# Two seven-product schemes extended: the row-kept 256-column groups of the first projection, and the last of the first experts

## The chip, the cores and the metric

One core of a Trainium2 chip runs the whole program. The metric is the device time of one execution in microseconds. A core has a matrix engine (TensorE, PE in the profile, with PEld for its weight loads), a vector engine (VectorE, DVE), a scalar engine (ScalarE, ACT), GpSimd (POOL) and a queue engine (SyncE, SP), which run their own instruction streams and meet at semaphores. Sixteen DMA engines move data; the transfers that SP issues are in one hardware queue (q1), those of GpSimd in a software queue (q0).

## The reference

The program computes two transformer-like layers over 2048 rows of width 1024, in float32. Two places matter here. In the first layer a projection feeds attention and a recurrence:

```python
hx = modulate(rmsnorm(x, norm1_w), sh1, sc1)          # 2048 rows
hc = modulate(rmsnorm(ctx, norm1_w), csh1, csc1)      # 256 context rows
aq, ak, av, mq, mk, mv, mo, gates = split(h @ w_in)   # widths 512 128 128 512 512 512 512 16
```

Its last step is a mixture of 16 experts; each takes the 256 rows that score highest for it:

```python
xg = h[bidx, idx]                       # 16 experts x 256 rows x 1024
g = einsum('becd,edf->becf', xg, w_gate); u = einsum('becd,edf->becf', xg, w_up)   # f = 512
y = einsum('becf,efd->becd', silu(g) * u, w_down) * gate[..., None]
out = zeros_like(h).at[bidx, idx].add(y)
```

The second layer begins with a projection of the result by `w_in_2` (1472 columns).

## The kernel before

**The scheme.** A product of two matrices, each cut into 2 by 2 blocks, can be made of seven block products instead of eight, with sums and differences of blocks made by DVE before (`make_left`, `make_right`) and joined after (`join`). The code names them P1 to P7. P1 is copied out of PSUM by ACT, the others are added by DVE onto what is already in SBUF; P7 is added twice.

**First projection** (`first_projection`, L427). Nine turns of 256 rows (two tiles j of 128) run: turn 0, seven "fast" turns (`fast_body`, L989 for PE and L758 for DVE) and the context turn. A turn makes 8 units of 256 columns by column (`fm`, L1006), kept by ACT, and then column groups kept by row, `TM1`: group 0 (512 columns), 1 (256), 2 (512), 3 (272, with the gates) and 4 (256). In the fast turns groups 0 and 2 are the two column halves of a seven-product scheme over the two row tiles and the two depth halves (L1014), four depth steps a product; groups 1, 3 and 4 are plain products of eight depth steps for each row tile (L1018), copied out by DVE (`keep_step`, L751). The order on PE is `STEPS` (L447). Three PSUM banks (`NB = 3`) serve all units in rotation, so that a step waits until the step three before it has been taken; the first three units of the next turn wait until all row-kept results of this turn are taken (L998). DVE's order is written out by hand: norm of the next rows, rotation of the previous turn's attention rows (`rotate`, L617), left and right blocks, and then the joins and copies with the eight convolutions of the previous turn (`convolve`, three instructions each, L705 and L707) and two additions of a modulation product (L398) between them. The right blocks lie in `right` and in the weights, where turn 0 overwrites group 0 of depth half 0 with `t3` at its end (L835). The context turn (`body`, L1030) makes four column units, and then groups 1, 2 and the gates for each tile.

**First experts** (`experts`, L3014). Expert 0 and expert 15 (`LAST`) are plain (`plain_up`, `plain_down`); experts 1 to 14 use seven products for gate and up (L3247, 3.57 us each) and seven for down (L3276, `down`). Beside the up products PE transposes the next expert's rows (L3202). GpSimd scatters each expert's two tiles of 128 rows into x with an accumulating indirect DMA (L3180). The blocks' scratch lies in the memory of the second projection's weights, `inp2_w`: SP loads these (`EarlyColumns.load`, L337, 5.9 MB in four transfers) once expert 14 is done (L3144). When the scatters have landed the stage ends with a barrier, and the second projection begins by loading rows of x, and waits for its weights at L4192 and L4167.

Of the kernel before, what the change touches and what calls it, by code (L numbers as in the profile page):

```python
# [10 lines left out]
ALU = mybir.AluOpType  # L11
# [317 lines left out]
class EarlyColumns:  # L329
# [7 lines left out]
    def load(self, sp):  # L337
        for k in range(0, KD, 4):
            sp.dma_start(self.w[:, k:k + 4, self.first:], self.view[:, k:k + 4, self.first:]).then_inc(self.fm_landed, 16)
        for k in range(0, KD, 4):  # L340
            sp.dma_start(self.w[:, k:k + 4, 0:self.first], self.view[:, k:k + 4, 0:self.first]).then_inc(self.tm_landed, 16)
# [85 lines left out]
def first_projection(nc, K, groups, first_weights, late_mod, rope, q_norm, k_norm, taps, tm_out, qT_out, kT_out, conv_out, tm_k,  # L427
# [18 lines left out]
    P1, P2, P6, P5, P3, P7, P4 = "P1", "P2", "P6", "P5", "P3", "P7", "P4"  # L446
# [3 lines left out]
    kept_order = [P2, (0, 1), (0, 3), (0, 4), (1, 1), P3, P7, (1, 3), (1, 4), P4]  # L450
    joined_order = [P6, P5, P7]
# [30 lines left out]
    with Stage(nc, "inp1") as s:  # L482
# [11 lines left out]
        left = s.sb("left", [P, 2, KH, P])  # L494
        o = s.sb("o", [P, TB, W])
# [16 lines left out]
                 "first_kept", "joined", "t3_made", "right_made", "left_made", "zeroed", "edged", "cch", "conved", "silued", "scaled", "y_stored", "k_turned", "k_kept", "k_stored", "gated", "passed")  # L512
        (dch, rooted, x_scaled, turned, hT_ready, unit, fm_kept, tm_kept,
         w_ready, squared, summed, q_rooted, qch, rotated, q_turned, q_kept, q_stored,
         first_kept, joined, t3_made, right_made, left_made, zeroed, edged, cch, conved, silued, scaled, y_stored, k_turned, k_kept, k_stored, gated, passed) = (s.sem(n) for n in names)
# [4 lines left out]
        b11, t3, b21, b22 = (w[:, depth * KH:(depth + 1) * KH, lo:lo + BANK]  # L520
                             for depth, lo in ((0, tm_chunks[2][0]), (0, tm_chunks[0][0]), (1, tm_chunks[2][0]), (1, tm_chunks[0][0])))
# [5 lines left out]
        def joint(j, c):  # L527

            return tm[:, j, tm_at[c]:tm_at[c] + BANK]

        def step_bank(step):
            return psU[:, step_at[step] % NB, :]
# [4 lines left out]
        def wait_taken(engine, g, step):  # L537

            if step == P1:
                engine.wait_ge(first_kept, g)  # L540
            elif step in joined_order:
                engine.wait_ge(joined, g * 3 - 3 + joined_order.index(step) + 1)
            else:
                engine.wait_ge(tm_kept, g * NT + kept_order.index(step) + 1)
# [59 lines left out]
        def _(dve):  # L604
# [107 lines left out]

            def make_left(g, par, n):
# [15 lines left out]
            def make_right(g, n):  # L729

                at_g = g * 4 - 4
                if n == 2:
                    dve.wait_ge(t3_made, 1)
                    ins = dve.tensor_tensor(right[:, :, :], t3, b11, ALU.add)
                else:
                    dve.wait_ge(right_made, at_g + (1 if n == 1 else 3))
                    ins = dve.tensor_tensor(right[:, :, :], b22 if n == 1 else b21, right[:, :, :], ALU.subtract)
                ins.then_inc(right_made, 1)

            def join(g, step, to, other, after, done):  # L740

                wait_made(dve, g, step)
                if after:
                    wait_taken(dve, g, after)
                dve.tensor_tensor(to, step_bank(step), other, ALU.add).then_inc(done, 1)  # L745

            def keep_step(g, step):
                j, c = step
                lo, n = tm_chunks[c]
                wait_made(dve, g, step)  # L750
                dve.tensor_copy(tm[:, j, tm_at[c]:tm_at[c] + n], step_bank(step)[:, 0:n]).then_inc(tm_kept, 1)  # L751
# [6 lines left out]
            def fast_body(g, par, following):  # L758
# [9 lines left out]
                dve.wait_ge(tm_stored[0], g * 16)  # L768
                join(g, P2, joint(0, 2), joint(1, 2), P1, tm_kept)
                convolve(b, other, 0)  # L770
                join(g, P6, joint(1, 2), joint(1, 2), P1, joined)
                make_right(g, 1)
                make_left(g, par, 4)
                keep_step(g, (0, 1))
                convolve(b, other, 1)
# [3 lines left out]
                dve.wait_ge(tm_stored[1], g * 16)  # L779
                join(g, P5, joint(1, 0), joint(1, 2), P6, joined)  # L780
                make_left(g, par, 3)
                keep_step(g, (0, 4))
                make_right(g, 2)
                keep_step(g, (1, 1))
                convolve(b, other, 3)
                make_right(g, 4)
                join(g, P3, joint(0, 0), joint(1, 0), P5, tm_kept)
                keep_gates(g, 0)
                convolve(b, other, 4)
                mod.add(dve, g + 1, 1, psT[:, 1, :])  # L790
                join(g, P7, joint(1, 0), joint(1, 0), P5, tm_kept)
                join(g, P7, joint(1, 2), joint(1, 2), P6, joined)
                convolve(b, other, 5)
                keep_step(g, (1, 3))
                convolve(b, other, 6)
                keep_step(g, (1, 4))
                convolve(b, other, 7)
                join(g, P4, joint(1, 2), joint(1, 2), P7, tm_kept)
# [3 lines left out]
            def body(g, par, following):  # L802
# [31 lines left out]
                if first_turn(g):  # L834
                    dve.tensor_tensor(t3, b22, t3, ALU.subtract).then_inc(t3_made, 1)  # L835
# [10 lines left out]
        def _(act):  # L846
# [58 lines left out]
            def body(g, par, following):  # L905
# [17 lines left out]
                if fast(g):  # L923
                    act.wait_ge(tm_stored[1], g * 16)
                    wait_made(act, g, P1)
                    act.activation(joint(1, 2), step_bank(P1), ACT.Copy).then_inc(first_kept, 1)
# [21 lines left out]
        def _(pe):  # L948
# [40 lines left out]
            def fast_body(g, par, following):  # L989
                lhs = {P1: rows_of(par, 0, 0), P2: rows_of(par, 1, 0), P6: left[:, 1, :, :], P5: left[:, 0, :, :],  # L990
                       P3: left[:, 1, :, :], P7: left[:, 0, :, :], P4: rows_of(par, 1, 1)}
                rhs = {P1: b11, P2: b21, P6: right[:, :, :], P5: right[:, :, :], P3: b22, P7: t3, P4: right[:, :, :]}
                pe.wait_ge(hT_ready, g * TB * 2 + TB * 2)
                for u in range(UW):
# [13 lines left out]
                    elif step in lhs:  # L1008
                        if step in (P6, P3, P7):
                            pe.wait_ge(left_made, g * 4 - 4 + {P6: 2, P3: 3, P7: 4}[step])  # L1010
                        if step in (P6, P5, P4):
                            pe.wait_ge(right_made, g * 4 - 4 + {P6: 1, P5: 2, P4: 4}[step])
                        for k in range(KH):
                            mm = pe.matmul(psU[:, u % NB, :], lhs[step][:, k, :], rhs[step][:, k, :], start=(k == 0), stop=(k == KH - 1))  # L1014
                    else:
                        j, (lo, n) = step[0], tm_chunks[step[1]]
# [4 lines left out]
                    if u + 1 in MOD_AFTER:  # L1021
                        r = MOD_AFTER.index(u + 1)
# [7 lines left out]
            def body(g, par, following):  # L1030
# [4140 lines left out]
```

## Time and profile before

| what | us |
|---|---|
| median of 3 runs (lowest, highest) | 3951.31 (3942.11, 3953.16) |
| the profiled execution's own time | 3947.6 |
| span of the profile | 3946.0 |
| PE busy | 3646.0 (92%) |
| DVE busy | 2497.9 (63%) |
| ACT busy | 1554.6 (39%) |
| mean granted TensorE clock | 0.964 of full |

The page gives the shares over the whole span; stages differ, so the views by stretch of time are what the argument rests on. In them each row is one instruction or a run of equal ones: start, duration, engine, line of the kernel, operation, what it writes and reads, count, and in brackets how long the engine had been idle before it and what ended the wait. Two starts on one engine give the time that a thing really takes up, since the durations of neighbours overlap by some hundredths.

### The profile page before, as it was taken

The page shows a single profiled execution, that of the slowest core. Times are in us where ns is not written, and L with a number is a line of the kernel's source. Part 1 is how long each engine was busy: PE and PEld are TensorE (multiplying, and loading weights), DVE is VectorE, ACT ScalarE, POOL GpSimd, SP SyncE. Part 2 cuts the span into 40 slices and gives each one's busy share as a digit, 9 for nine tenths or more (in the row PEclk, how much of TensorE's full clock was granted, in tenths as well). Part 3 has the DMA queues.
Part 4 walks back from the last instruction along what each step waited for, and adds up shares of the span by engine and source line. Part 5 has one row for each costly group of instructions (what it writes and reads, how often), then busy time and mean ns, then how long its engine had stood idle before and what let it go on. Part 6 is the DMA issues. An engine that isn't in the chain of part 4 may idle for free. (4 is left out here: it accounts for less than half of the span.)

```text
span 3946.0 us, 65209 instructions
## 1 busy us (share of the span) xinstructions
PE 3646.0 (92%) x22959; PEld 2415.7 (61%) x22960; DVE 2497.9 (63%) x4701; ACT 1554.6 (39%) x3424; POOL 682.2 (17%) x802
## 2 busy tenths in 40 slices
PE   6999999699898977999999899998999999599998
PEld 4667776455594434888787677765666555344444
DVE  1456556556488754787874487785333566678886
ACT  1122221355563432222121467664333233367765
POOL 0000000100173220212120010110000132322222
PEclk8999999899999988999999899998999999699999
DMA  6122222222435568767664221224240143598974
GB/s 247 67 91 85 73 90 70 90 74 82 126 121 188 174 251 314 226 203 225 215 214 152 68 66 62 64 65 122 67 133 16 37 153 118 211 325 267 332 240 101
DMA packets 227211, 574.59 MB, mean 146 GB/s; under 512 B 28154, under 2 KB 100986, under 8 KB 211118
## 3 DMA queue, kind: packets, MB, share of 16 engines
q1 hardware_dynamic: 177742, 395.92, 28.6%
q0 software_dynamic: 49248, 175.79, 15.3%
q8 instruction: 130, 2.13, 0.2%
q14 instruction: 91, 0.75, 0.1%
HBM read 433.59 MB, written 137.93 MB: 145 GB/s over the span
## 5 line engine op out<-in xcount | busy, mean ns | idle before, releaser
L4959 DVE COPY moe_bu<-moe_wu 128x1024 f32 x480 | 298.9, 698 | 38.8 <-DMA moe_wd<-in_w_down 21.7
L4846 PE MATMUL moe_psU<-moe_bu,shared_weights 128*32 128x256 f32 x3840 | 295.1, 382 | 1.4 <-issue 1.3
L4846 PE MATMUL moe_psU<-moe_wu,shared_weights 128*32 x1280 | 293.2, 382 | 1.5 <-DVE moe_bu L4959 1.3
L4175 PE MATMUL inp_psU<-shared_weights,inp_w 128*128 128x256 f32 x1024 | 231.9, 382 | 2.8 <-DMA inp_wg<-in_lru_wx 2.8
L4175 PEld LDWEIGHTS inp_psU<-shared_weights,inp_w 128*128 128x128 f32 x1024 | 195.1, 192 | 35.8 <-issue 10.2
L4915 ACT ACTIVATE moe_bd<-moe_wd 128x1024 f32 x200 | 198.0, 1048 | 28.8 <-PE moe_psD L4868 28.8
L4846 PEld LDWEIGHTS moe_psU<-moe_wu,shared_weights 128*32 128x32 f32 x1280 | 134.3, 110 | 111.5 <-issue 12.5
L1006 PE MATMUL inp_psU<-inp_hT,inp_w 128*128 128x256 f32 x896 | 197.2, 380 | 5.5 <-DVE inp_tm L745 4.9
L1006 PEld LDWEIGHTS inp_psU<-inp_hT,inp_w 128*128 128x128 f32 x896 | 168.7, 190 | 32.9 <-DVE inp_tm L745 6.4
L1501 DVE TENSOR_SCALAR_CACHE_REDUCE att_junk<-att_psS,att_snk 128x640 f32<-128x640 f32 x128 | 108.1, 882 | 108.8 <-PE att_psS L1420 108.8
L4868 PE MATMUL moe_psD<-moe_bd,moe_hT 128*32 128x512 f32 x960 | 153.2, 595 | 0.0
L1018 PE MATMUL inp_psU<-inp_w,inp_hT 128*128 128x256 f32 (+1 forms) x672 | 152.6, 384 | 0.0
L4846 PEld LDWEIGHTS moe_psU<-moe_bu,shared_weights 128*32 128x32 f32 x3840 | 151.2, 110 | 1.6 <-issue 1.6
L4868 PE MATMUL moe_psD<-moe_wd,moe_hT 128*32 x320 | 151.1, 595 | 1.1 <-ACT moe_hT L4912 0.5
L3180 POOL DMA_INDIRECT x<-moe_y,moe_at_out x32 | 68.3, 2136 | 482.2 <-DVE moe_y L3467 414.8
L1547 ACT ACTIVATE att_p<-att_psS,att_low 128x640 f32<-128x640 f32 x128 | 101.3, 793 | 119.2 <-DVE att_junk L1501 97.8
L1018 PEld LDWEIGHTS inp_psU<-inp_w,inp_hT 128*128 128x128 f32 x672 | 126.6, 190 | 25.4 <-issue 6.7
L4898 ACT ACTIVATE shared_weights<-moe_psT,mod_cols,mod_scale 128x128 f32<-128x128 f32 x320 | 120.4, 458 | 48.9 <-PE moe_psT L4834 48.9
L3457 DVE TENSOR_TENSOR inp_w<-moe_ps,inp_w 128x512 f32<-128x512 f32 x84 | 58.1, 692 | 104.4 <-PE moe_ps L3247 102.9
L3313 ACT ACTIVATE moe_xT<-moe_psT,mod_cols,mod_scale 128x128 f32<-128x128 f32 x256 | 95.5, 457 | 70.9 <-PE moe_psT L3202 70.8
L4502 ACT ACTIVATE lata_pT<-lata_psP 128x512 f32<-128x512 f32 (+3 forms) x112 | 61.2, 549 | 157.7 <-PE lata_psP L4402 157.7
L4451 DVE TENSOR_TENSOR lata_psS<-lata_psS,lata_mask 128x128 f32<-128x128 f32 x64 | 19.0, 297 | 159.4 <-PE lata_psS L4392 159.4
(805 smaller groups left out, 8590.5 us busy)
## 6 DMA issues: line engine op xcount, KB each, us to landing
moe_wu<-in_w_up SPq DMA_DIRECT2D x32, 2048.0 KB
moe_d_w<-in_w_down SPq DMA_DIRECT2D x16, 2048.0 KB, 13.2
moe_wd<-in_w_down SPq DMA_DIRECT2D x32, 1024.0 KB
moe_u_w<-in_w_up SPq DMA_DIRECT2D x15, 2048.0 KB, 14.0
mod_w<-in_w_ada SPq DMA_DIRECT2D x24, 1024.0 KB, 12.0
inp_mod_w<-in_w_mod SPq DMA_DIRECT2D x16, 1024.0 KB, 4.8
xn<-out_xn POOLq DMA_DIRECT2D x32, 512.0 KB, 4.4
shared_weights<-in_w_gate SPq DMA_DIRECT2D x8, 2048.0 KB, 8.9
```

Source lines behind the costliest of these rows:

```text
L1006: mm = pe.matmul(psU[:, u % NB, 0:G], w[:, k, fm_lo + u * P:fm_lo + (u + 1) * P], hT[:, par, k, :], start=(k == 0), stop=(k == KD - 1))
L1018: mm = pe.matmul(psU[:, u % NB, 0:n], hT[:, par, k, j * P:(j + 1) * P], w[:, k, lo:lo + n], start=(k == 0), stop=(k == KD - 1))
L1501: dve.tensor_scalar(junk[:, kv, :], psS[:, kv, LO:LO + KEYS], 1.0, snk[:, 1, h:h + 1], ALU.mult, ALU.min, accum_out=low[:, j, h:h + 1]).th ...
L1547: act.activation(p[:, g % 2, kv, :], psS[:, kv, LO:LO + KEYS], ACT.Exp, scale=-1.0, bias=low[:, j, h:h + 1], accum_out=sums[:, j, h:h + 1] ...
L3180: pool.indirect_dma_start(out=target, out_offset=bass.IndirectOffsetOnAxis(ap=at_out[:, p, r:r + 1], axis=0), in_=y[:, p, r, :], in_offset ...
L3313: ins = act.activation(xT[:, e % 2, k, r * P:(r + 1) * P], psT[:, h, (k % 4) * P:(k % 4 + 1) * P], ACT.Identity, scale=scale2[k], bias=shi ...
L4175: mm = pe.matmul(psU[:, m % 2, u % 2 * G:(u % 2 + 1) * G], w[:, k, TM2_W + u * P:TM2_W + (u + 1) * P], hT[:, par, k, :], start=(k == 0), s ...
L4846: mm = pe.matmul(psU[c, f, 0:2 * P], xT[:, p, k, c], w, start=(k == 0), stop=(k == KD - 1), tile_position=(0, g * LOT))
L4868: mm = pe.matmul(psD[c, n, :], hT[:, f, c], w, start=(f == 0), stop=(f == FB - 1), tile_position=(0, g * LOT))
L4898: ins = act.activation(xT[:, p, k, :], psT[:, q, (k % 4) * P:(k % 4 + 1) * P], ACT.Identity, scale=scale2[k], bias=shift2[k])
L4915: return act.activation(bd[:, g - 1, f, :].unsqueeze(1), wd[:, bass.ds(slot, 1), f, :], ACT.Copy)
L4959: ins = dve.tensor_copy(bu[:, g - 1, f, c, :].rearrange("p k n -> p (k n)").unsqueeze(1), wu[:, bass.ds(slots[g - 1], 1), f, c, :].rearran ...
```

## The change

In the fast turns of the first projection groups 1 and 4 become the column halves of a second seven-product scheme (`SLIM`, 256 columns a half) beside the first one (`WIDE`, 512). Its right blocks take the place of the rotation's scratch `qsq`, and its `t3` overwrites group 4 of depth half 0; the gates' 16 columns of the region read by the context turn are saved before and put back in the context turn, whose row-kept units wait for it. DVE's order is new. In the experts the last one also uses seven products, and the second projection's weights are loaded in two halves by depth, the first when the last expert's up products are done, the second when its down products are.

```diff
-    STEPS = [P1, P2, P6, (0, 1), (0, 3), P5, (0, 4), (1, 1), P3, P7, (1, 3), (1, 4), P4]
+    STEPS = [(P1, WIDE), (P2, WIDE), (P1, SLIM), (P2, SLIM), (P6, WIDE), (P6, SLIM), (0, 3), (P5, WIDE), (P5, SLIM), (1, 3),
+             (P3, WIDE), (P3, SLIM), (P7, WIDE), (P7, SLIM), (P4, WIDE), (P4, SLIM)]
+    MOD_FAST = (NF + 4, NF + 12)
...
+        rights = right[:, :, :], qsq[:, :, :].rearrange("p j n -> p (j n)")[:, 0:KH * 256].rearrange("p (k n) -> p k n", k=KH)
+        t3_gates = t3[SLIM][:, :, 240:256]
...
-                make_right(g, 2)
+                make_right(g, WIDE, 2)
+                make_right(g, SLIM, 2)
                 dve.wait_ge(fm_kept, g * NF + NF)
                 edges(b, other, False)
...
+                join(g, (P2, WIDE), 0, 0, 0, tm_kept, P1)
                 convolve(b, other, 0)
+                join(g, (P2, SLIM), 0, 0, 0, tm_kept, P1)
+                join(g, (P6, WIDE), 1, 0, 0, joined, P1)
+                make_right(g, WIDE, 1)
+                join(g, (P6, SLIM), 1, 0, 0, joined, P1)
+                make_right(g, SLIM, 1)
                 make_left(g, par, 4)
                 keep_step(g, (0, 3))
                 mod.add(dve, g + 1, 0, psT[:, 0, :])
+                join(g, (P5, WIDE), 1, 1, 0, joined, P6)
+                convolve(b, other, 1)
+                join(g, (P5, SLIM), 1, 1, 0, joined, P6)
+                make_left(g, par, 3)
+                make_right(g, WIDE, 3)
+                keep_step(g, (1, 3))
+                make_right(g, WIDE, 4)
+                join(g, (P3, WIDE), 0, 1, 1, tm_kept, P5)
+                make_right(g, SLIM, 3)
+                make_right(g, SLIM, 4)
+                join(g, (P3, SLIM), 0, 1, 1, tm_kept, P5)
+                dve.wait_ge(tm_kept, g * NT + kept_order.index((P3, SLIM)) + 1)
+                keep_gates(g, 0)
                 convolve(b, other, 2)
+                join(g, (P7, WIDE), 1, 1, 1, tm_kept, P5)
+                join(g, (P7, WIDE), 1, 0, 0, joined, P6)
                 convolve(b, other, 3)
+                join(g, (P7, SLIM), 1, 1, 1, tm_kept, P5)
+                join(g, (P7, SLIM), 1, 0, 0, joined, P6)
+                mod.add(dve, g + 1, 1, psT[:, 1, :])
                 convolve(b, other, 4)
                 convolve(b, other, 5)
+                join(g, (P4, WIDE), 1, 0, 0, tm_kept, P7)
                 convolve(b, other, 6)
+                join(g, (P4, SLIM), 1, 0, 0, tm_kept, P7)
                 convolve(b, other, 7)
...
                     rotate(g - 1, 1 - par)
+                    dve.tensor_copy(t3_gates, gates_quadrant[:, :, :]).then_inc(quadrant_saved, 1)
...
+                    dve.tensor_tensor(t3[WIDE], b22[WIDE], t3[WIDE], ALU.subtract).then_inc(t3_made, 1)
+                    dve.tensor_copy(gates_quadrant[:, :, :], t3_gates).then_inc(quadrant_saved, 1)
+                    dve.wait_ge(quadrant_saved, 1)
+                    dve.tensor_tensor(t3[SLIM], b22[SLIM], t3[SLIM], ALU.subtract).then_inc(t3_made, 1)
...
+                    act.wait_ge(rotated, g * 4 * TB)
+                    for pair in (WIDE, SLIM):
+                        wait_made(act, g, (P1, pair))
+                        act.activation(joint(pair, 1, 0), step_bank((P1, pair)), ACT.Copy).then_inc(first_kept, 1)
...
+                    if u == NF and is_ctx(g):
+                        pe.wait_ge(quadrant_saved, 2)
...
     def plain(e):
-        return e in (0, LAST)
+        return e == 0
...
-            sp.wait_ge(made, base(LAST))
-            next_columns.load(sp)
+            sp.wait_ge(made, made_by(LAST, P4))
+            next_columns.load_half(sp, 0)
+            sp.wait_ge(made, made_by(LAST, P4, True))
+            next_columns.load_half(sp, 1)
...
-            for e in range(1, LAST):
+            for e in range(1, units):
                 up(e)
                 down(e)
-            plain_up(LAST)
-            plain_down(LAST)
```

## Rows read from the trace of the kernel before

**Rows 1.** The page: PE's busy time, share of the span and instructions.

```profile
PE 3646.0 (92%) x22959; PEld 2415.7 (61%) x22960; DVE 2497.9 (63%) x4701; ACT 1554.6 (39%) x3424; POOL 682.2 (17%) x802
```

**Rows 2.** One fast turn by windows: length, busy time of each engine, clock, DMA share, GB/s.

```profile
375.00:454.92 79.92, 79.14 (x331) 56.70 (x331) 46.66 (x87) 18.32 (x39) 5.00 (x8) 1.00 0.23 83
```

**Rows 3.** Timeline of PE in that turn, and the next turn's first row.

```profile
412.66 3.60 PE L1014 MATMUL inp_psU<-inp_right,inp_left 128*128 128x512 f32 x8
416.09 3.62 PE L1018 MATMUL inp_psU<-inp_w,inp_hT 128*128 128x256 f32 x16
419.64 1.06 PE L388 MATMUL inp_psT<-inp_mod_w,inp_mod_cb 128*32 128x512 f32 x8
...
450.54 3.60 PE L1014 MATMUL inp_psU<-inp_right,inp_hT 128*128 128x512 f32 x8
454.92 10.63 PE L1006 MATMUL inp_psU<-inp_hT,inp_w 128*128 128x256 f32 x48 [0.78 <-DVE inp_tm L745]
```

**Rows 4.** Timeline of DVE in the same turn.

```profile
404.22 0.17 DVE L695 COPY inp_fm<-inp_fm 128x8 f32<-128x8 f32 x1 [5.23 <-ACT inp_fm L913]
...
416.90 2.28 DVE L737 TENSOR_TENSOR inp_right<-inp_w,inp_right 128x2048 f32<-128x2048 f32 x1
...
419.75 0.43 DVE L751 COPY inp_tm<-inp_psU 128x256 f32<-128x256 f32 x1
420.09 0.35 DVE L705 TENSOR_SCALAR inp_y<-inp_fm,inp_tap 128x256 f32<-128x256 f32 x1
...
441.02 0.35 DVE L705 TENSOR_SCALAR inp_y<-inp_fm,inp_tap 128x256 f32<-128x256 f32 x1
...
442.33 0.68 DVE L398 TENSOR_TENSOR inp_mod_row<-inp_mod_row,inp_psT 128x512 f32<-128x512 f32 x1
443.62 1.29 DVE L745 TENSOR_TENSOR inp_tm<-inp_psU,inp_tm 128x512 f32<-128x512 f32 x2 [0.61 <-PE inp_psU L1014]
...
454.17 0.69 DVE L745 TENSOR_TENSOR inp_tm<-inp_psU,inp_tm 128x512 f32<-128x512 f32 x1 [1.71 <-PE inp_psU L1014]
```

**Rows 5.** Timeline of the context turn: PE's first row-kept unit.

```profile
710.92 3.62 PE L1068 MATMUL inp_psU<-inp_w,inp_hT 128*128 128x256 f32 x16
```

**Rows 6.** Timeline of the context turn: DVE, the rotation's last and a later copy.

```profile
713.35 0.22 DVE L652 TENSOR_TENSOR inp_o<-inp_t 128x64 f32<-128x64 f32 x1
...
734.60 0.69 DVE L822 COPY inp_tm<-inp_psU 128x512 f32<-128x512 f32 x1 [1.66 <-PE inp_psU L1068]
```

**Rows 7.** Timeline of PE: expert 14 (first rows), start of expert 15.

```profile
2087.53 7.31 PE L3247 MATMUL moe_ps<-moe_xT,shared_weights 128*128 128x128 f32 x64
2094.67 0.60 PE L3202 MATMUL moe_psT<-ident,moe_xg 128*128 128x128 f32 x4
2095.11 3.74 PE L3247 MATMUL moe_ps<-inp_w 128*128 128x128 f32 x32
...
2126.30 3.62 PE L3224 MATMUL moe_ps<-moe_xT,moe_g_w 128*128 128x256 f32 x16
```

**Rows 8.** Timeline of POOL: expert 14's second scatter, expert 15's second.

```profile
2129.40 1.55 POOL L3180 DMA_INDIRECT x<-moe_y,moe_at_out  x1 [1.95 <-DVE moe_y L3467]
...
2170.62 1.55 POOL L3180 DMA_INDIRECT x<-moe_y,moe_at_out  x1 [5.33 <-DVE moe_y L3370]
```

**Rows 9.** Timeline of SP and PE: the second projection's first rows.

```profile
2177.77 0.82 SPq L3638 DMA_DIRECT2D shared_rows<-x  x2
...
2192.89 20.00 PE L4175 MATMUL inp_psU<-shared_weights,inp_w 128*128 128x256 f32 x80 [2.79 <-DMA inp_wg<-in_lru_wx]
```

**Rows 10.** DMA issues near the end of expert 13: size, us from issue to landing.

```profile
moe_d_w<-in_w_down SPq DMA_DIRECT2D x1, 2048.0 KB, 12.8
x<-moe_y,moe_at_out POOLq DMA_INDIRECT x1, 10.6
```

**Rows 11.** DMA issues, 2080 to 2200 us: the second projection's weights.

```profile
inp_w<-in_w_in SPq DMA_DIRECT2D x2, 896.0 KB, 20.5
```

**Rows 12.** DMA issues, 2169 to 2173 us: the last scatter.

```profile
x<-moe_y,moe_at_out POOLq DMA_INDIRECT x1, 5.9
```

More of the change, by code:

```diff
@@ L335, in __init__, with load_half @@
         self.fm_landed, self.tm_landed = nc.alloc_semaphore(f"{name}_fm_landed"), nc.alloc_semaphore(f"{name}_tm_landed")
[L337 to L341, printed above, removed]
+    def load_half(self, sp, n):
+        k = 4 * n
+        sp.dma_start(self.w[:, k:k + 4, self.first:], self.view[:, k:k + 4, self.first:]).then_inc(self.fm_landed, 16)
+        sp.dma_start(self.w[:, k:k + 4, 0:self.first], self.view[:, k:k + 4, 0:self.first]).then_inc(self.tm_landed, 16)
 class LateModulation:
@@ L537, in wait_taken @@
         def wait_taken(engine, g, step):
[L539 to L542, printed above, removed]
+            if step[0] == P1:
+                engine.wait_ge(first_kept, g * 2 - 1 + step[1])
+            elif step in joined_order and step not in kept_order or step[0] == P7:
+                engine.wait_ge(joined, g * 6 - 6 + joined_order.index(step) + 1)
             else:
@@ L711, in convolve @@
                 ins.then_inc(conved, 1)
+            right_order = [(WIDE, 2), (SLIM, 2), (WIDE, 1), (SLIM, 1), (WIDE, 3), (WIDE, 4), (SLIM, 3), (SLIM, 4)]
             def make_left(g, par, n):
@@ L727, in make_left, with make_right, join @@
                 ins.then_inc(left_made, 1)
[L729 to L734, printed above, removed]
[L735 to L737 removed]
+            def make_right(g, pair, n):
+                at_g = g * 8 - 8 + right_order.index((pair, n))
+                to = rights[pair]
+                if n in (2, 3):
+                    dve.wait_ge(t3_made, pair + 1)
+                    ins = dve.tensor_tensor(to, t3[pair], b11[pair], ALU.add)
+                else:
+                    dve.wait_ge(right_made, g * 8 - 8 + right_order.index((pair, n - 1 if n == 4 else 2)) + 1)
+                    ins = dve.tensor_tensor(to, b22[pair] if n == 1 else b21[pair], to, ALU.subtract)
                 ins.then_inc(right_made, 1)
[L740 removed]
+            def join(g, step, j, half, other, done, after):
+                pair = step[1]
                 wait_made(dve, g, step)
[L743 to L745 removed]
+                if after == P1:
+                    dve.wait_ge(first_kept, g * 2 - 1 + pair)
+                else:
+                    dve.wait_ge(joined, g * 6 - 6 + joined_order.index((after, pair)) + 1)
+                dve.tensor_tensor(joint(pair, j, half), step_bank(step), joint(pair, 1, other), ALU.add).then_inc(done, 1)
             def keep_step(g, step):
[L748 to L749 removed]
                 wait_made(dve, g, step)
[L751 removed]
+                dve.tensor_copy(tm[:, step[0], tm_at[3]:tm_at[3] + 272], step_bank(step)).then_inc(tm_kept, 1)
             def keep_gates(g, j):
@@ L764, in fast_body @@
                 make_left(g, par, 2)
-                make_right(g, 2)
+                make_right(g, WIDE, 2)
+                make_right(g, SLIM, 2)
                 dve.wait_ge(fm_kept, g * NF + NF)
                 edges(b, other, False)
-                dve.wait_ge(tm_stored[0], g * 16)
-                join(g, P2, joint(0, 2), joint(1, 2), P1, tm_kept)
+                for j in range(TB):
+                    dve.wait_ge(tm_stored[j], g * 16)
+                join(g, (P2, WIDE), 0, 0, 0, tm_kept, P1)
@@ L1124, in put_tm @@
             def put_tm(g, j):
-                pool.wait_ge(tm_kept, g * NT + (kept_order.index(P3) + 1 if fast(g) and j == 0 else (j + 1) * NC))
+                pool.wait_ge(tm_kept, g * NT + (kept_order.index((P3, SLIM)) + 1 if fast(g) and j == 0 else (j + 1) * NC))
                 hi = tm_at[3] if is_ctx(g) else TM1_W
@@ L3335, in _ @@
             silu_plain(0)
-            for e in range(1, LAST):
+            for e in range(1, units):
                 if e > 1:
@@ L3478, in _ @@
             make_x_right(1, 3)
-            for e in range(1, LAST):
+            for e in range(1, units):
                 keep_gates(e)
```

79 lines of the change are left out of this document (31 added, 48 removed).

## The prediction

> **What bounds the kernel now.** The page comes first: PE is busy for 92% of the span, DVE for 63% [rows 1]. The table by windows then shows whether this holds where the change is: in a fast turn of the projection PE works 79.14 of 79.92 us at the full granted clock, DVE 46.66 [rows 2]. Third, the timeline of PE: the only pause is 0.78 us at the turn's start, ended by DVE's last join, that of P4 [rows 3]. So a shorter PE turn shortens the kernel, as long as DVE stays behind PE by no more than it does now; what DVE has queued when PE ends a turn is what to look at. In the experts PE's work is one row after another [rows 7] until the last expert; after it comes no PE work but a chain: last weighing on DVE, scatter by GpSimd, landing, barrier, loading of rows [rows 8, 9].
>
> **PE in a fast turn.** Removed are four plain products: the 16 instructions of one take 419.64 - 416.09 = 3.55 us from start to start, 0.222 each [rows 3]; four are 14.20. Added are seven slim products of 8 such instructions, 1.775 each: 12.43. PE's work shrinks by 1.77 us. Seven wide products (3.43 each, 416.09 - 412.66) stay. PE would end P4 SLIM at 450.54 + 3.43 - 1.77 = 452.20, on the old turn's scale.
>
> **DVE's tail.** Going backwards from 452.20: P4 SLIM 1.77, P4 WIDE 3.43, P7 SLIM 1.77, so P7 WIDE ends at 445.23 and its join starts 0.2 later (the old P4's: ended 453.97, join at 454.17 [rows 3, 4]), at 445.4. From there DVE has, in its written order, the following. Two wide joins: 1.29 for both, less overlap 1.21. One convolution: 442.33 - 441.02 = 1.31. Two slim joins: a copy of 256 columns out of PSUM takes 0.34 from start to start and 0.43 in itself; the trace has no slim join, so I take the copy's 0.34, since a wide join's 0.69 is what a 512-column addition [rows 4] takes too; 0.68. The modulation's addition 0.60 (0.68 less overlap). Two convolutions 2.62. The wide P4 join 0.61. One convolution 1.31. That adds up to 8.34: the last join starts at 453.75 and ends after 0.43 at 454.18; PE starts 0.06 after such an end (454.17 + 0.69 = 454.86 against 454.92). The new turn begins at 454.24, not 454.92: 0.68 us are gained, and PE idles 2.04 us in place of 0.78. Convolutions 4 to 6 stand between PE's last products and the joins that release the next turn; before, DVE had 1.71 us of idleness there [rows 4]. Seven turns give **4.8 us**.
>
> Does DVE arrive at 445.4 in time? P3 WIDE ends at 441.8 - 1.0 (modulation product, 1.06 less overlap [rows 3]) - 1.77 = 439.0. Then follow its join (0.61, from 439.2), two slim right blocks, the P3 SLIM join, gates 0.3, one convolution. A slim right block has 1024 elements; between 0.69 for 512 and 2.28 for 2048 lies 1.22, less overlap 1.14. The sum ends at 444.0, so 1.4 us are spare. Further back, the wide right block (2.20) and then the slim join, slim right block and left block between P6 and P5 end about 426, while P5 SLIM begins about 430: covered. At the turn's front, DVE now idles 5.23 us before the edges [rows 4]; one slim block (1.14) and the convolution and gates that slip behind the last join (about 1.1 us later relative to PE) fit in. The turn-0 additions (copy and second t3, about 1.4 us) fit there too. If that cover were gone, PE would wait for P2's join by what exceeds it. ACT's later silu, one convolution later, delays only column units that have two banks in hand. The modulation's second product comes eight steps after the first, not four, with its load between, so it waits less.
>
> A rule of the Trainium skill speaks against the halves: "VectorE: DVE Perf Modes", section "The TRN2 errata", says that an instruction reading SBUF pays a fixed time whatever its size, and advises tiles of 512 or more. If each of the three slim joins in the tail cost its full 0.43, the turn would gain 0.4 and not 0.7 us, and the total below would be 2 us higher; the 0.34 from start to start is the trace's, and decides.
>
> **The context turn.** PE reaches its first row-kept unit at 710.92 without a wait [rows 5]. It now waits for the copy that puts the gates' columns back, which DVE issues behind the whole rotation; that ends at 713.57 [rows 6]. With 0.2 for the copy and 0.06 for the release, PE starts at 713.8: 2.9 us later. Behind it stand all its row-kept units, and DVE waits for them (1.66 us before the copy at 734.60 [rows 6]), so nothing gives it back. The bounds are 0 (only if DVE's other work were what bounds the end) and 3.5. I take **2.9 lost**.
>
> **The last expert.** Expert 14 takes 2126.30 - 2087.53 = 38.77 us of PE, of which four transposes (2095.11 - 2094.67 = 0.44 each, 1.76) fall away for the last [rows 7]: 37.0, so PE ends at 2163.3. The second scatter of expert 14 was issued 3.10 us after PE's end (2129.40 against 2126.30 [rows 7, 8]); so this one is issued at 2166.4, 4.2 us before the old 2170.62. The old one landed in 5.9 [rows 12], at 2176.5, and the stage ended 1.25 later with the first row loads at 2177.77 [rows 9]. But the second half of the weights, 2.94 MB, is now issued at about 2163.5, and a scatter beside such a load takes 10.6 us [rows 10]. That gives 2177.0, stage end 2178.25: **0.5 us lost**, where the PE side promised 4.2.
>
> The weights of the half: 2 MB beside two scatters landed in 12.8 [rows 10], or 0.25 MB/us with the scatters' 1.05 MB counted; all 5.9 MB, the last part issued at 2128, landed at 2148.5 with two scatters [rows 11], 0.31 MB/us. So 4 MB take 12.7 to 16 us and end at 2176 to 2179.7. The row loads are issued behind them in the same queue at 2178.25 and may start up to 1.4 us late; PE's first products had waited 2.79 us for another load [rows 9], which covers it. The bounds of this part are -4.2 (no slowing) and +4 (the half ends 4 us after my latest, beyond cover).
>
> The Trainium skill's "DMA: Bandwidth & Descriptors", section "Queues, rings and completion order", says that each DMA engine takes turns between the queues that have work, a packet at a time. With the two queues sharing evenly, a scatter of 5.9 us would take up to twice that, 11.8, and the stage would end 1.2 us later than by the 10.6 used here; the rows agree with the rule.
>
> **Sum.** 3947.6 - 4.8 + 2.9 + 0.5 = 3946.2 against the profiled execution's own time. That execution was 3.7 us under the median of the three runs; the same difference on the median gives 3949.9. I put the time between, at 3948.
>
> **Rivals.**
> *DVE keeps up.* If DVE's tail did not bind, the last join would start at 452.4, and the turn gain 454.92 - 452.85 = 2.07 us, 14.5 in all: 3947.6 - 14.5 + 2.9 + 0.5 = 3936.5, and 3931.8 if the scatter isn't slowed either. For it: DVE is idle 33 us a turn. Against: eight operations written between P7's end and P4's last join. Chance 0.20.
> *The scatter is not slowed,* the rest as forecast: 3947.6 - 4.8 + 2.9 - 4.2 = 3941.5. For it: the weights' first rows may be over when it starts. Against: rows 10. Chance 0.12.
> *Slower: slim operations on DVE cost as much as wide ones.* Then the two slim right blocks add 2 x 1.06, which uses up the 1.4 spare and starts the tail 0.7 late, and the slim joins add 2 x 0.27 + 0.26: the turn begins at 455.7, 0.8 later than before. It decides once the tail is over 0.7 longer than I have it. Seven turns lose 5.6, so 3947.6 + 5.6 + 2.9 + 0.5 = 3956.6, and 3960.6 with the late weights. Against: the copy of 256 takes 0.43, not 0.69. Chance 0.15.
> *The change doesn't shorten PE:* if a slim product took a wide one's 3.43, a turn would grow by 7 x 3.43 - 14.2 = 9.8: 4016. The 256-column row excludes nearly all of it. Chance 0.03.
> The forecast has 0.50.
>
> **How the numbers follow.** What can be told from no change is 0.3%, 11.8 us. The forecast, the quick scatter and most of the others lie within it: 0.77. Faster by more takes DVE keeping up and a bit beside: 0.15. Slower by more takes the slow rival with late weights, or the last: 0.08. The range, 3936 to 3957, goes from the first rival to the third, and holds what the runs of before spread.
>
> **What would show it.** In the changed profile: fast turns of about 79.2 us, with PE idle about 2 us at each start, ended by a DVE join, and DVE without a gap between P7's joins and P4's; PE idle near 3 us in the context turn before its first row-kept unit, ended by the copy of the gates' columns; a last expert of 37 us on PE, its last scatter landing in 10 to 11 us, and the second projection's first row load within a microsecond of where it was. I am wrong if the turns are 78 us (or 80 and more), or if that load comes 4 us earlier.

## The result and the profile after

| | before | changed |
|---|---|---|
| median of 20 runs of each | 3947.46 us | 3954.39 us |
| ratio, 95% interval | | 1.0016 [1.0009, 1.0023] |
| profiled execution: own time, span | 3947.6, 3946.0 | 3952.9, 3951.3 |

The change costs 4 to 9 us (the interval of the ratio) where the forecast said 1.4 less for the profiled execution. One run of the changed kernel took 6384.9 us at a mean granted clock of 0.61; it is not in the ratio, and without it the median is 3954.37. The line of the page that answers to [rows 1]; columns as there:

```profile
PE 3640.3 (92%) x22995; PEld 2411.2 (61%) x22996; DVE 2565.2 (65%) x4779; ACT 1557.7 (39%) x3431; POOL 685.3 (17%) x802
```

PE is busy 5.7 us less, and yet the kernel is longer. I went through both timelines by the same marks:

| stretch (us) | before | changed | difference | forecast |
|---|---|---|---|---|
| turn 1 to context turn, first product to first product | 558.78 | 557.89 | -0.9 | -4.8 |
| context turn, first product to first row-kept unit | 16.01 | 20.51 | +4.5 | +2.9 |
| from there to expert 15's first product | 1415.4 | 1417.5 | +2.1 | 0 |
| expert 15's start on PE to the second projection's row load | 51.47 | 51.80 | +0.3 | +0.5 |
| from that row load to the end of the span | 1768.2 | 1767.3 | -0.9 | 0 |

With 0.15 us ahead of turn 1 these make the 5.3 us of the spans. The last expert came out near the forecast (+0.3 for +0.5). The 0.9 us gained in the last stretch lie at its start: from the row load to the second projection's first product it takes 14.18 us, before 15.12. That product waited 2.79 us for another load before [rows 9]; now it waits 1.77 for ACT. The loss is in the projection. The timeline of PE in the changed kernel shows the projection's turns (start, length, engine, line, operation; in brackets the idle time before and who ended it):

```profile
294.00 10.63 PE L1037 MATMUL inp_psU<-inp_hT,inp_w 128*128 128x256 f32 x48 [1.90 <-DVE inp_tm L763]
373.32 12.31 PE L1037 MATMUL inp_psU<-inp_hT,inp_w 128*128 128x256 f32 x48 [1.90 <-DVE inp_tm L763]
454.32 10.63 PE L1037 MATMUL inp_psU<-inp_hT,inp_w 128*128 128x256 f32 x48 [1.90 <-DVE inp_tm L763]
533.72 12.29 PE L1037 MATMUL inp_psU<-inp_hT,inp_w 128*128 128x256 f32 x48 [1.99 <-DVE inp_tm L763]
694.17 8.83 PE L1098 MATMUL inp_psU<-inp_hT,inp_w 128*128 128x256 f32 x32 [2.00 <-DVE inp_tm L763]
...
714.68 5.41 PE L1102 MATMUL inp_psU<-inp_w,inp_hT 128*128 128x256 f32 x16 [2.64 <-DVE inp_w L834]
```

The turn from 294.00 takes 79.32 us, as forecast (79.24), with 1.90 idle at its start (2.04). But the 48 matmuls at 373.32 and 533.72 take 12.31 and 12.29 us and not 10.63; the 32 of the context turn take 8.83 where the kernel before has 7.14, and the 16 behind the new 2.64 us wait take 5.41 and not 3.62 [rows 5]. In four places the same instructions take longer, by 1.68, 1.66, 1.69 and 1.79: 6.8 us together. The table by windows says why (window, length, busy PE, granted clock, DMA share, GB/s):

```profile
373.30:375.00 1.70, 1.68 (x6) 0.79 0.00 0
375.00:377.00 2.00, 2.00 (x6) 0.50 0.74 303
377.00:380.00 3.00, 3.00 (x14) 0.88 0.09 30
453.00:458.00 5.00, 3.68 (x17) 1.00 0.29 120
...
696.20:698.20 2.00, 2.00 (x6) 0.50 0.33 133
716.50:718.50 2.00, 2.00 (x6) 0.50 0.00 0
```

The granted clock is at 0.50, the 1.2 GHz level, for a few microseconds shortly after the pause; there the matmuls start about twice as far apart. At 454, behind a pause as long, it stays at 1.00. In the kernel before it is 1.00 over the fast turn [rows 2], its start included.

### The profile page after: what moved, and what is told of

The parts are those of the page before. It is cut to its first block and busy times, and to the rows that moved or that the text cites. A ratio compares the mean times of both kernels' runs of the same rounds, so it can differ in the third digit from the quotient of the medians.

```text
span 3951.3 us, 65537 instructions
## 1 busy us (share of the span) xinstructions
PE 3640.3 (92%) x22995; PEld 2411.2 (61%) x22996; DVE 2565.2 (65%) x4779; ACT 1557.7 (39%) x3431; POOL 685.3 (17%) x802
## 5 line engine op out<-in xcount | busy, mean ns | idle before, releaser
L763 DVE TENSOR_TENSOR inp_tm<-inp_psU,inp_tm 128x512 f32<-128x512 f32 (+1 forms) x98 | 53.1, 554 | 132.4 <-PE inp_psU L1046 132.4
L4841 POOL DMA_INDIRECT out_rows<-shared_weights,moe_at_out x40 | 64.8, 1620 | 272.9 <-DVE shared_weights L4983 202.2
```

Source lines behind the costliest of these rows:

```text
L4841: pool.indirect_dma_start(out=out, out_offset=bass.IndirectOffsetOnAxis(ap=at_out[:, p, :], axis=0), in_=y[:, p, :], in_offset=None, compu ...
```

## The experiments

**The pause theory:** PE's new pauses of 1.9 to 2.6 us sometimes let the granted clock fall to 1.2 GHz for a few microseconds of work after, and that is what ate the gain. **Rivals:** the slim products themselves (their DVE work, their weight loads); the DMA load that runs there; DVE in arrears from turn to turn. The kernel before was run beside each batch: median 3949.51 beside the first four, 3946.78 beside the next four, 3947.84 beside the last two; so ratios are compared, and places within the profiles. A run's later stages vary by some microseconds (the output stage, from the first reload of its columns to the issue of the next modulation's weights, took 217.8 to 221.5 us in the twelve profiles, its code the same in all), which a median alone doesn't separate. The clock goes along with that too. Windows of that stage's start in two of the kernels below, first in both, where the stage is 3.1 us shorter, then in best; columns as above:

```profile
1186.00:1206.00 20.00, 16.46 (x36) 0.84 0.92 307
1206.00:1226.00 20.00, 16.99 (x45) 0.91 0.32 108
...
1246.00:1266.00 20.00, 16.82 (x68) 1.00 0.55 189
```

```profile
1186.00:1206.00 20.00, 16.99 (x36) 0.78 0.84 285
1206.00:1226.00 20.00, 16.68 (x39) 0.83 0.41 129
...
1246.00:1266.00 20.00, 16.61 (x60) 0.91 0.46 161
```

**tail.** On DVE the P4 join of the wide scheme is moved ahead of one convolution (5), that of the slim scheme ahead of two (5 and 6); convolution 7 stood behind both already:

```diff
                 mod.add(dve, g + 1, 1, psT[:, 1, :])
                 convolve(b, other, 4)
+                join(g, (P4, WIDE), 1, 0, 0, tm_kept, P7)
+                join(g, (P4, SLIM), 1, 0, 0, tm_kept, P7)
                 convolve(b, other, 5)
-                join(g, (P4, WIDE), 1, 0, 0, tm_kept, P7)
                 convolve(b, other, 6)
-                join(g, (P4, SLIM), 1, 0, 0, tm_kept, P7)
                 convolve(b, other, 7)
```

> The changed kernel with DVE's last convolutions (5, 6, 7) of a fast turn moved behind both P4 joins. Pause theory: a pause of 1.9 to 2.0 us of PE at a turn's start lets the granted clock drop to 0.5 in some turns (three of seven in the profile of the changed kernel), which costs 1.7 us each time. The pause shrinks by 1.33 to about 0.6 us, all seven starts are fast, turns take about 77.9 us: 3952.9 - 7 x 1.33 - 3 x 1.7 = 3938.5. Rival, slim products: the slow starts come from what PE computed before (the slim products), not from the pause: the pauses shrink, slow starts stay, 3943.6. Rival, backlog: the convolutions only push DVE's delay to the front of the next turn, PE waits there instead, no gain: 3952.

Measured 3940.45 (3938.34 to 3943.26), ratio 0.9981 [0.9972, 0.9990]. The turns are 77.9 us, and no start is slow. PE's timeline in it, a fast turn's start, the context turn's, and its first row-kept unit:

```profile
369.97 10.63 PE L1037 MATMUL inp_psU<-inp_hT,inp_w 128*128 128x256 f32 x48 [0.52 <-DVE inp_tm L763]
681.91 7.14 PE L1098 MATMUL inp_psU<-inp_hT,inp_w 128*128 128x256 f32 x32 [0.61 <-DVE inp_tm L763]
...
700.71 3.72 PE L1102 MATMUL inp_psU<-inp_w,inp_hT 128*128 128x256 f32 x16 [2.63 <-DVE inp_w L834]
```

The slim products are all there, and cost what PE's count said: 79.92 - 77.9 = 2.0 us a turn are gained, near the 2.07 of my rival "DVE keeps up". So neither they nor their DVE work are enough to make slow starts. The 2.63 us wait is still there and this time is followed by 3.72 us at a granted clock of 1.00: a pause makes a fall possible, not certain.

**copy_first.** The copy that puts the gates' columns back goes ahead of the rotation:

```diff
+                    dve.wait_ge(tm_kept, g * NT)
+                    dve.tensor_copy(t3_gates, gates_quadrant[:, :, :]).then_inc(quadrant_saved, 1)
                     rotate(g - 1, 1 - par)
-                    dve.tensor_copy(t3_gates, gates_quadrant[:, :, :]).then_inc(quadrant_saved, 1)
```

> The changed kernel with the copy of the gates' columns moved ahead of the rotation in the context turn. Pause theory: the wait of 2.64 us goes, and with it the slow first row-kept product (5.41 instead of 3.62 us): 4.4 us less, 3948.5. Rival, slim products or the context turn itself makes it slow: the product stays at 5.4, 2.6 us less, 3950.3. Rival, DVE bounds the context turn's end: nothing gained, 3952.9.

Measured 3951.55 (3948.57 to 3954.86), ratio 1.0007 [0.9998, 1.0016]. The first row-kept unit has no wait and full speed, 3.62 us; its place in the context turn moves from 20.51 to 17.70 us, and with the slow product the edit gives 4.6 us. By the medians (a ratio of 1.0007 against 1.0016) it is 3.6 us, which doesn't separate the 4.4 I expected from the 2.6 of the rival; the places do. The three slow starts at 373.95, 534.35 and 694.78, behind pauses of about 2 us, all stay:

```profile
694.78 8.83 PE L1099 MATMUL inp_psU<-inp_hT,inp_w 128*128 128x256 f32 x32 [1.99 <-DVE inp_tm L763]
...
712.48 3.62 PE L1103 MATMUL inp_psU<-inp_w,inp_hT 128*128 128x256 f32 x16
```

**pad.** The kernel before, without any slim product, with two more operations on DVE that only take time, so that PE waits longer at each turn's start:

```diff
                 convolve(b, other, 7)
+                for n in range(2):
+                    dve.tensor_tensor(qsq[:, :, :], qsq[:, :, :], qsq[:, :, :], ALU.max).then_inc(padded, 1)
+                    dve.wait_ge(padded, g * 2 - 1 + n)
                 join(g, P4, joint(1, 2), joint(1, 2), P7, tm_kept)
```

> The kernel before, without any slim product, with two additional DVE operations on 1280 elements (about 1.45 us each, values unchanged) ahead of the P4 join, so that PE's pause at each turn's start grows from 0.8 to about 2.0 us. Pause theory: the turns grow by 1.2 us, and some of the seven starts after them are slow, 1.7 us each: 3947.6 + 8.4 + 1.7 to 5.1 = 3957.7 to 3961. Rival, slim products: all starts stay fast: 3956.0.

Measured 3964.75 (3961.24 to 3969.07), ratio 1.0045 [1.0031, 1.0058]. The pauses are 2.04 to 2.29 us, and two of seven starts are slow:

```profile
300.12 10.63 PE L1009 MATMUL inp_psU<-inp_hT,inp_w 128*128 128x256 f32 x48 [2.19 <-DVE inp_tm L745]
381.45 12.21 PE L1009 MATMUL inp_psU<-inp_hT,inp_w 128*128 128x256 f32 x48 [2.19 <-DVE inp_tm L745]
```

So the kernel before does it too, given the pause. The rival of the slim products is out for a second time. The median is above the 3957.7 to 3961 that I had set: from the start at 218.78 to the context turn's the six turns take 11.4 us more than before (8.1 of pauses, 3.3 of two slow starts), and the rest of the difference is elsewhere and unexplained.

**projection_only.** The changes to the first projection without those to the experts.

> The first projection's part of the change alone, the experts as before. If the whole loss is in the projection, as the stage marks of the two profiles say (+5.5 us at the end of the projection, +0.3 in the experts): about 5 us over the kernel before, 3952.6. If the experts' part were what costs: 3947.

Measured 3949.62 (3945.47 to 3953.34), ratio 1.0003 [0.9994, 1.0012]. Its projection is the changed kernel's: slow starts at 373.88, 534.28, 694.71 and 715.21, and the last transposes of the modulation's row on PE 605.32 us after turn 1's start, 599.97 before, 5.35 more. The median shows next to nothing of these 5 us: the ratio is 1.3 per mille lower than the changed kernel's, and its interval includes 1. Part of that is later stages: from the second projection's row load to the end this profile took 1760.6 us, that of before 1768.2, of the changed kernel 1767.3. Whether all of it is, this run doesn't say.

**experts_only.** The experts' part alone.

> The kernel before with the experts' part of the change alone (the last expert like the others, the next weights in two halves). By my step: PE ends the last expert about 4 us earlier, but the last scatter lands in 10.4 us beside the second half of the weights instead of 5.9, so the row loads of the second projection are issued 0.3 to 0.5 us later than before: 3949.8 (3949 to 3951). Rival (the scatter isn't what sets the end of the stage): 4.2 less, 3945.3. Rival (late weights hold back the second projection's first rows): 2 to 4 us more there, 3952 to 3954.

Measured 3947.02 (3941.42 to 3950.45), ratio 1.0000 [0.9991, 1.0009]. From the issue of expert 14's gate weights, my mark for this stage, to the second projection's row load it takes 141.13 us, before 140.84: +0.3, as in the changed kernel (141.18). The last scatter in it lands in 10.3 us. The experts' part costs next to nothing and gives nothing.

**half_late.** The changed kernel, the second half of the weights only once the scatters have landed:

```diff
             sp.wait_ge(made, made_by(LAST, P4, True))
+            for p in range(2):
+                sp.wait_ge(stored[p], STORES * units // 2)
             next_columns.load_half(sp, 1)
```

> The changed kernel, with the second half of the next weights loaded only once all scatters have landed. If the load beside it is what stretches the last scatter, it lands in about 6.0 us instead of 10.4, and the stage ends some 4.3 us earlier in relation to PE's last product; then 2.94 MB of weights stand ahead of the row loads, 9.5 us at 0.31 MB/us, so that the second projection's first product comes about 3 us later than in the changed kernel: 3957. Rival (a scatter at the end takes 10 us whatever lies beside it): landing stays at 10.4, and the whole loses 7 us or more: 3962.

Measured 3952.22 (3947.38 to 3955.79), ratio 1.0013 [1.0003, 1.0022], against 1.0016 for the changed kernel; so the 3 us more that I expected of the whole don't show. In the place itself it is as expected. The last scatter by the DMA issues (kind and count, median us from issue to landing), first in the changed kernel, then here:

```profile
x<-moe_y,moe_at_out POOLq DMA_INDIRECT x1, 10.4
```

```profile
x<-moe_y,moe_at_out POOLq DMA_INDIRECT x1, 6.0
```

The row load comes 137.51 us after the same mark instead of 141.18, and the first product of the second projection 158.21 instead of 155.36, 2.9 later, behind the weights. The total doesn't show it, for which two things can stand: the two intervals overlap widely, and later stages were shorter in this profile (568.7 us from the last router's bias load to the end, 571.0 in the changed kernel's). This run has the changed kernel's projection unaltered, but its slow starts are at other turns:

```profile
291.84 12.31 PE L1037 MATMUL inp_psU<-inp_hT,inp_w 128*128 128x256 f32 x48 [1.90 <-DVE inp_tm L763]
372.84 10.63 PE L1037 MATMUL inp_psU<-inp_hT,inp_w 128*128 128x256 f32 x48 [1.90 <-DVE inp_tm L763]
452.15 12.31 PE L1037 MATMUL inp_psU<-inp_hT,inp_w 128*128 128x256 f32 x48 [1.90 <-DVE inp_tm L763]
...
612.63 12.29 PE L1037 MATMUL inp_psU<-inp_hT,inp_w 128*128 128x256 f32 x48 [2.00 <-DVE inp_tm L763]
693.70 7.14 PE L1098 MATMUL inp_psU<-inp_hT,inp_w 128*128 128x256 f32 x32 [2.00 <-DVE inp_tm L763]
```

It is again every second one. So what runs in a particular turn isn't the cause, nor are arrears that build up: those would come back in the same turn.

**both.** The edits of tail and copy_first together.

> The changed kernel with both earlier edits: P4's two joins ahead of convolutions 5 to 7 on DVE, and in the context turn the copy of the gates' columns ahead of the rotation. Pause theory: the turns stay at 77.9 us and their starts at 0.5 us of idleness; the 2.6 us pause in the context turn goes, and with it the half-clock product of 1.8 us behind it. Against P4's joins moved alone (3940.5) that is 4.4 less: 3936. From the context turn's start to the last modulation's mark it should take about 41.2 us, as before the change, and the x32 group at its start 7.14. Rival (the slow products belong to the slim products or to the load of the turn, not to pauses): a slow product stays in the context turn, 3938; if the pause merely moves to a later wait there, 3940.

Measured 3933.77 (3932.65 to 3936.23), ratio 0.9969 [0.9957, 0.9981]. All starts at full speed, the first row-kept unit 16.01 us into the context turn as before the change. This is faster than the kernel before by 7 to 17 us.

**filler.** The changed kernel; while PE would stand idle at a fast turn's end, it transposes the identity:

```diff
                         turn_q(g - 1, (u - NF - 1) // 2)
+                pe.wait_ge(q_kept, g * 3)
+                for n in range(12):
+                    mm = pe.transpose(psX[:, (n % 4) * P:(n % 4 + 1) * P], K["ident"][:, :], K["ident"][:, :])
```

> The changed kernel, and TensorE does 12 transposes of the identity (0.13 us each, 1.6 us) at the end of each fast turn, while it would stand idle for DVE's last join; their result is used nowhere. Nothing that the turn waits for is moved, so a turn stays at 79.3 us with 0.3 to 0.5 us of idleness instead of 1.9 to 2.0. Pause theory: what lowered the granted clock was TensorE standing still, so the starts of the turns at 373, 534 and of the context turn are no longer slow (10.6, 10.6 and 7.1 us instead of 12.3, 12.3 and 8.8): 5.1 less than the changed kernel, 3949.3; the slow product behind the 2.6 us pause in the context turn stays. Rival (the slow starts come from the turn's length or from what else runs then, not from the pause): all stay, 3954.4. Rival (the fillers come in the way of the last join or of the next turn): turns of over 79.6.

Measured 3949.82 (3945.17 to 3954.81), ratio 1.0004 [0.9995, 1.0013]. PE's timeline around a turn's start, at the context turn's, and its first row-kept unit:

```profile
213.42 1.47 PE L1063 MATMUL inp_psX<-ident 128*128 128x128 f32 x12
215.48 10.63 PE L1037 MATMUL inp_psU<-inp_hT,inp_w 128*128 128x256 f32 x48 [0.59 <-DVE inp_tm L763]
...
691.57 7.14 PE L1101 MATMUL inp_psU<-inp_hT,inp_w 128*128 128x256 f32 x32 [0.69 <-DVE inp_tm L763]
710.38 5.41 PE L1105 MATMUL inp_psU<-inp_w,inp_hT 128*128 128x256 f32 x16 [2.64 <-DVE inp_w L834]
```

This is the cleanest test: DVE's order, the transfers and the join that ends the wait are the changed kernel's, the turns stay at 79.3 us, and PE does more work. None of the seven starts is slow, and turn 1's start to the context turn's takes 554.50 us against 557.89: 3.4 less, and 1.69 more at the context turn's own start. The pause that wasn't filled, 2.64 us, is still followed by a slow product. The cause is PE standing still, not DVE's tail as such. By the ratios (1.0004 against 1.0016) the whole gains 4.7 us, near the 5.1 expected.

**pad_long.** As pad, with four operations in place of two.

> The kernel before with four extra DVE operations of 1.5 us (two in the earlier trial) in front of P4's join in each fast turn: 4.4 us more per turn than before, idleness at the start 5.1 us instead of 0.8. Seven turns add 30.5: 3980 without slow starts. Pause theory: every start behind so long a pause may be slow (1.7 us each), at least the 2 of 7 seen behind pauses of 2.1 us and up to all 8: 3983 to 3993. Rival (whether a start is slow hangs on the pause's place and not on its length): 2 slow again, 3983; rival (pauses have nothing to do with it): 3980.

Measured 3996.97 (3993.78 to 3999.63), ratio 1.0125 [1.0110, 1.0141]; more than any of the theories said. The pauses are 5.1 to 5.3 us, and all seven starts are slow; the timeline of the first and the longest of them, then the windows behind one pause:

```profile
219.61 12.94 PE L1009 MATMUL inp_psU<-inp_hT,inp_w 128*128 128x256 f32 x48 [5.09 <-DVE inp_tm L745]
...
392.33 13.61 PE L1009 MATMUL inp_psU<-inp_hT,inp_w 128*128 128x256 f32 x48 [5.24 <-DVE inp_tm L745]
```

```profile
651.90:655.90 4.00, 4.00 (x10) 0.50 0.58 225
655.90:657.90 2.00, 2.00 (x6) 0.52 0.99 342
657.90:660.90 3.00, 3.00 (x15) 1.00 0.06 21
```

The loss per start is 1.4 to 3.0 us. From 219.61 to the context turn's start at 739.10 the six turns take 519.5 us, 39.7 more than before: 26.4 of that are pauses (4.4 each), 13.3 the six slow starts. I had set 3983 to 3993, at most 1.7 a start; behind the longer pause the seven starts lose 2.2 on average.

**best.** Both DVE edits, and the next weights in three parts; some scratch blocks of the experts change places for it, which isn't shown here:

```diff
-            sp.wait_ge(made, made_by(LAST, P4))
-            next_columns.load_half(sp, 0)
-            sp.wait_ge(made, made_by(LAST, P4, True))
-            next_columns.load_half(sp, 1)
+            sp.wait_ge(made, made_by(LAST, P3))
+            next_columns.load_part(sp, 0, 4)
+            sp.wait_ge(mixed, 2 * LAST)
+            next_columns.load_part(sp, 4, 6)
+            sp.wait_ge(made, made_by(LAST, P3, True))
+            sp.wait_ge(d_right, 4 * LAST)
+            next_columns.load_part(sp, 6, 8)
```

> Both DVE edits, and the next weights in three parts by depth (4, 2 and 2 of the 8 blocks), issued in the last expert after the up product P3, behind the mixing, and after the down product P3. The projection's part as in the kernel with both DVE edits, 3936. In the last expert less is left to load when the last scatter starts (2 of 8 blocks, 1.5 MB, and it issued some us ahead, not 2.9 MB), so it should land in 6 to 8 us instead of 10.4: 3 to 4 us less, 3932.6. Rival (a scatter is slowed by whatever is loading when it starts, however little is left): 3936.

Measured 3929.36 (3922.80 to 3932.46), ratio 0.9953 [0.9939, 0.9967]: 13 to 24 us faster than the kernel before. The last scatter by the DMA issues, then SP's second and third part and the row load in its timeline:

```profile
x<-moe_y,moe_at_out POOLq DMA_INDIRECT x1, 6.3
```

```profile
2143.39 0.37 SPq L338 DMA_DIRECT2D inp_w<-in_w_in  x1
...
2150.45 0.37 SPq L338 DMA_DIRECT2D inp_w<-in_w_in  x1
...
2164.43 0.81 SPq L3672 DMA_DIRECT2D shared_rows<-x  x2
```

The third part is issued 6.3 us ahead of the last scatter (2156.79), and its two transfers land in 4.8 us (1024 KB) and 5.6 us (448 KB): it is over when that starts. The row load comes 137.15 us after the issue of expert 14's gate weights (141.23 in both), 4.1 less, and the second projection's first product 151.98 against 155.38: 3.4 gained, since that product now waits 2.47 us for another load.

## Why the prediction was wrong

- **PE in a fast turn, right.** Tail's turns gain 1.99 us where PE's count alone gave 2.07 (2.03, with the 0.43 of the last join and the 0.06 behind it added as in my own sum).
- **DVE's tail, right.** DVE's timeline in the changed kernel has no gap from P7's joins at 285.25 to P4's last, and my sum of it is right to within 0.1 us. The last join was to start 8.34 us after the first:

```profile
285.25 1.29 DVE L763 TENSOR_TENSOR inp_tm<-inp_psU,inp_tm 128x512 f32<-128x512 f32 x2 [1.02 <-PE inp_psU L1046]
...
287.76 0.75 DVE L763 TENSOR_TENSOR inp_tm<-inp_psU,inp_tm 128x256 f32<-128x256 f32 x2
...
291.63 0.68 DVE L763 TENSOR_TENSOR inp_tm<-inp_psU,inp_tm 128x512 f32<-128x512 f32 x1
...
293.53 0.42 DVE L763 TENSOR_TENSOR inp_tm<-inp_psU,inp_tm 128x256 f32<-128x256 f32 x1
```

  It starts 8.28 after. The slim joins cost 0.33 from start to start, the wide ones 0.60 to 0.61; the rival of dear slim operations is out, and half the columns cost little more than half the time.
- **"0.68 us are gained, and PE idles 2.04 us in place of 0.78": the step that failed.** I priced the idle time at its own length, and put what it does to the work behind it at nothing, without a reason. In the changed kernel's profile three of seven such pauses are followed by a stretch at 1.2 GHz that costs another 1.7 us: 3.4 in the seven turns, 1.7 at the context turn's start. Without that the seven turns give 4.2 us of my 4.8; with it 0.9 is left.
- **The context turn, right in its wait (2.64 against 2.9), short by the same thing.** The product behind that pause takes 1.8 us more, at a granted clock of 0.50; no term of the sum had it.
- **The last expert, right.** +0.3 for +0.5, the scatter in 10.4 us for 10.6; half_late and best show that the load beside it is what stretches it. So my rival of the scatter that isn't slowed is out.
- **The sum.** My 3946.2 and 6.8 of slow clock make 3953.0; the profile has 3952.9. That this agrees to 0.1 is partly luck: the 0.9 us gained behind the row load, which I hadn't forecast, make up for errors of the other sign.
- **The forecast of "no change within 0.3%"** held for the size (0.16%), but the sign, a small loss, was not in my forecast; the one rival on that side (slim DVE operations as dear as wide ones, 3956.6) came near in time by another mechanism.

What in the profile before could have told me? At the turns' starts each pause was 0.78 to 0.88 us and the clock full, and I took a longer pause for one more of the same kind. But the same profile has longer ones elsewhere. At the end of the projection PE works without a gap at a granted clock of 1.00 (730 to 738 us), stands still for 3.38 us, and then makes eight transposes in 1.97 us that take 1.07 at 736.10; the timeline, then the window:

```profile
741.65 1.97 PE L1097 MATMUL inp_psT<-ident,inp_x 128*128 128x128 f32 x8 [3.38 <-ACT inp_x L879]
```

```profile
741.60:743.60 2.00, 1.95 (x8) 0.50 0.71 272
```

And the 80 matmuls behind the 2.79 us wait of [rows 9], which I used only as cover, take 20.00 us, where at 0.222 each they would take 17.8; the windows of their first 4 us show 0.50. (There PE had worked only 5.3 of the 25 us ahead, so that row doesn't show the wait alone to be the reason.) So the profile before priced a pause of 3 us at more than its length, but has nothing on one of 2 us. I should have put the unknown in as a term between 0 and what the matmuls of a start lose at the lower level. The first 16 of them alone take 3.6 us at full clock and would take twice that.

## What to carry to other kernels

Where an edit shortens an engine that was nearly gapless and leaves a pause of 2 us in its place, count the pause and, beside it, a possible fall of TensorE's clock behind it: here 1.7 us a time, at three of seven starts. See first whether what ends the pause can be moved forward in its engine's order: two joins written one and two convolutions earlier were worth 14 us here, where the change itself had given none. Where a transfer at a stage's end is stretched by a bulk load beside it, issue the load in parts, so that little of it is left when the transfer starts.

## What the runs showed of the hardware

Granted clock behind one pause of PE in an 80 us turn that is otherwise without gaps, by the starts of seven turns in each profile:

| profile | pause, us | slow of 7 | loss each, us |
|---|---|---|---|
| tail, both, best | 0.52 to 0.61 | 0 in each | 0 |
| filler | 0.59 to 0.69 | 0 | 0 |
| before, experts_only | 0.78 to 0.88 | 0 in each | 0 |
| changed, projection_only, copy_first, half_late | 1.89 to 2.00 | 3 in each | 1.7 |
| pad | 2.04 to 2.29 | 2 | 1.6 to 1.7 |
| pad_long | 5.09 to 5.34 | 7 | 1.4 to 3.0 |

At 1.9 to 2.0 us it is every second start, though which ones differs from run to run; with pad's longer turns two, three turns apart. The 2.64 us pause in the context turn was followed by a slow product in four profiles of five (changed, projection_only, half_late, filler), not in tail. A pause of 1.05 us in the context turn (ahead of the transposes at 707.00 in the kernel before) stands in all twelve profiles, and the product behind it has full speed in each, 3.62 us. The 3.38 us pause at the projection's end was followed by slow transposes in eight of twelve (1.95 to 1.97 us in seven, 1.54 in copy_first), by fast ones (1.09) in tail, both, filler and half_late. What decides which of two equal pauses is followed by the fall, and where between 1.05 and 1.9 us it begins, stays open: pad and pad_long changed the turns' length along with the pause, and no turn's start has a pause between 0.88 and 1.89.
